# Two transformer blocks on one core: the order of rotary, convolutions and weight splits ahead of the scan loop

## The reference

```python
hn = rmsnorm_2(x, norm_mix_g[layer])
proj = hn @ w_in[layer]
u_pool, m_q, m_k, m_v, m_o, m_i, m_f, a_q, a_k, a_v = jnp.split(proj, offsets, axis=-1)
y_pool = pool_mixer(u_pool, pool_w[layer], pool_scale[layer])
y_mlstm = mlstm_mixer(m_q, m_k, m_v, m_o, m_i + gb[:n_gate], m_f + gb[n_gate:],
                      mlstm_conv_w[layer], mlstm_norm_g[layer])
y_attn = attn_mixer(a_q, a_k, a_v, q_norm_g[layer], k_norm_g[layer], cos, sin)
x = x + jnp.concatenate([y_pool, y_mlstm, y_attn], axis=-1) @ w_out[layer]
x = x + mem_cross_attn(rmsnorm_2(x, norm_mem_g[layer]), mem, ca_wq[layer], ca_wkv[layer], ca_wo[layer])
x = x + ec_moe(rmsnorm_2(x, norm_ffn_g[layer]), router_w[layer], expert_w_gu[layer], expert_w_down[layer])
```

## Time and profile before

| | |
|---|---|
| median of 3 runs | 1495.85 us (1495.27 to 1496.95) |
| profiled execution | 1495.81 us |
| its span | 1494.0 us |
| busy: PE, PEld | 1156.1, 779.3 us |
| busy: DVE, ACT, POOL | 443.3, 379.1, 69.3 us |
| DMA | 503.37 MB, mean 337 GB/s |

### The profile page before, as it was taken

How to read it: one execution, slowest core, us unless ns; L and a number is a source line. 1 busy time by engine, 2 the same in 40 slices (tenths; PEclk the granted TensorE clock), 3 DMA queues, 4 the chain that set the end, 5 groups by cost and what they waited for, 6 DMA issues and landing times.

```text
span 1494.0 us, 20251 instructions
## 1 busy us (share of the span) xinstructions
PE 1156.1 (77%) x8876; PEld 779.3 (52%) x8876; DVE 443.3 (30%) x879; ACT 379.1 (25%) x836; POOL 69.3 (5%) x83
## 2 busy tenths in 40 slices
PE   9999999999998997897556567566665665675677
PEld 8998989999976875442223223223222232232234
DVE  5555777545678854010000000000000000000002
ACT  5655566444555644110000000000000000000002
POOL 0000020000033411000000000000000000000000
PEclk9999999999998998898778787877777787877888
DMA  8435546555553388999999999999999999999996
GB/s 316 166 138 202 197 170 233 204 198 198 198 179 119 104 341 362 376 434 441 426 437 429 431 434 433 436 431 430 436 427 440 425 438 429 434 433 432 428 421 275
DMA packets 29164, 503.37 MB, mean 337 GB/s; under 512 B 4114, under 2 KB 4754, under 8 KB 8084
## 3 DMA queue, kind: packets, MB, share of 16 engines
q1 hardware_dynamic: 25200, 493.43, 79.4%
q10 hardware_dynamic: 3876, 8.65, 1.7%
HBM read 501.02 MB, written 1.05 MB: 336 GB/s over the span
## 4 chain that ended last, share of the span: by engine, by line
issue 63%; PE 31%; DVE 3%; ACT 2%; POOL 1%; DMA 0%; POOLq 0%; DVEq 0%; ACTq 0%
PE PB L99 30%; PE PB L102 1%; DVE SPL L108 1%; ACT SPH L105 1%; POOL SPL L108 0%; DVE XN L116 0%; DVE AQK L108 0%; DMA RAW<-in_wst_dram 0%; POOL SM L136 0%; POOL SP L112 0%; ACT XN L105 0%; DVE SM L128 0%; ACT SP L105 0%; DVE XQL L108 0%; DVE RT L108 0%
## 5 line engine op out<-in xcount | busy, mean ns | idle before, releaser
L99 PE MATMUL PB<-RING,XS 128*32 128x512 f32 x2048 | 297.6, 731 | 173.8 <-DMA RING<-in_wgu_dram 170.0
L99 PEld LDWEIGHTS PB<-RING,XS 128*32 128x32 f32 x2048 | 69.3, 128 | 347.3 <-DMA RING<-in_wgu_dram 185.2
L99 PE MATMUL PB<-RING,HHT 128*32 128x256 f32 x2048 | 152.3, 456 | 108.9 <-DMA RING<-in_wdn_dram 106.6
L108 DVE TENSOR_TENSOR SPL<-RAW,SPH 128x512 fp32r<-128x512 f32 x316 | 209.0, 719 | 42.3 <-ACT SPH L105 40.1
L99 PE MATMUL PB<-XTH,SPL 128*128 128x256 f32 x704 | 201.7, 287 | 0.0
L99 PE MATMUL PB<-XTH,SPH 128*128 128x256 f32 x704 | 199.2, 283 | 0.0
L99 PE MATMUL PB<-XTL,SPH 128*128 128x256 f32 x704 | 199.1, 283 | 0.0
L105 ACT ACTIVATE SPH<-RAW 128x512 fp32r<-128x512 f32 x340 | 186.8, 621 | 12.1 <-DMA RAW<-in_wst_dram 5.3
L99 PEld LDWEIGHTS PB<-RING,HHT 128*32 128x32 f32 x2048 | 72.2, 130 | 173.7 <-DMA RING<-in_wdn_dram 110.6
L105 ACT ACTIVATE SG<-PB 128x512 f32<-128x512 f32 (+1 forms) x21 | 11.9, 566 | 510.0 <-PE PB L99 508.7
L99 PEld LDWEIGHTS PB<-XTL,SPH 128*128 128x128 f32 x704 | 135.0, 192 | 0.5
(11 more groups left out here) (315 smaller groups left out, 1353.7 us busy)
## 6 DMA issues: line engine op xcount, KB each, us to landing
RAW<-in_wst_dram SPq DMA_DIRECT2D x84, 1024.0 KB, 4.8
RING<-in_wgu_dram SPq DMA_DIRECT2D x13, 2048.0 KB, 40.5
RING<-in_wgu_dram SPq DMA_DIRECT2D x14, 1024.0 KB, 9.0
RING<-in_wdn_dram SPq DMA_DIRECT2D x6, 2048.0 KB, 13.5
RING<-in_wgu_dram SPq DMA_DIRECT2D x2, 4096.0 KB, 19.5
RING<-in_wdn_dram SPq DMA_DIRECT2D x2, 4096.0 KB, 17.9
RING<-in_wdn_dram SPq DMA_DIRECT2D x3, 1024.0 KB, 42.8
RAW<-in_wst_dram SPq DMA_DIRECT2D x4, 256.0 KB, 5.6
```

Of the source, the lines that this page charges most:

```text
L99: return pe.do(lambda e: e.matmul(out_, lhsT, rhs, start=start, stop=stop), after)
L108: return on.do(lambda e: e.tensor_tensor(out_, a, b, op), after)
```

## The change

The tiles SP_ of the first two (step 0 and 2) move over AQK, those of the others to 139 and 141 KB. The generator `conv` now stops ahead of its tanh and once more at its end. Blocks 0 and 2 are convolved together, behind the first tile of the product for u and v; their tanh is emitted behind the copies of the second tile and of the transposes. Blocks 1 and 3 follow in step 0 of the loop, behind `attn_norm`. Three calls of `bg(4, 2)` are gone, one stands behind the first convolutions' end, and `bg(4, 1)` in the loop is `bg(6, 2)`. The exponentials of step 0 don't wait for `qk_ok[3]` any more.

```diff
--- before.py
+++ after.py
@@ -242,7 +242,7 @@
     BC = place("BC", [P, T], F32, at(194))
     MS = place("MS", [P, T], F32, at(195))
     NAC = place("NAC", [P, 2, P], F32, at(196))
-    SP_ = [place(f"SP{i}", [P, 512], F32, at(135 + 2 * i)) for i in range(4)]
+    SP_ = [place(f"SP{i}", [P, 512], F32, at(kb)) for i, kb in enumerate((151.5, 153.5, 139, 141))]
     ST_ = [place(f"ST{i}", [P, 512], F32, at(119 + 2 * i)) for i in range(4)]
 
     CQ = place("CQ", [P, 4, T], F32, at(119))
@@ -1090,21 +1090,20 @@
         for j in range(1, 5):
             c = [stt(CO[:, b, :], CI[:, b, j:j + T], CW[:, b, j:j + 1], CO[:, b, :], ALU.mult, ALU.add, ci)
                  for b, ci in zip(bs, c)]
+        yield
         a = [act(QK[:, b, :], CO[:, b, :], ACT.Tanh, ci, ffn_done, scale=0.5) for b, ci in zip(bs, c)]
         for b, ai in zip(bs, a):
             qk_ok[b] = stt(QK[:, b, :], QK[:, b, :], 1.0, CO[:, b, :], ALU.add, ALU.mult, ai)
+        yield
 
     conv_product(0)
     bg(4, 2)
     conv_product(1)
     m1, m2, mt = next(gates)
-    bg(4, 2)
     turn_qk(0, r0, (2, 3))
     conv_product(2)
     conv_product(3)
-    bg(4, 2)
     r1 = next(rot1)
-    bg(4, 2)
 
 
     def turn_gates():
@@ -1126,10 +1125,12 @@
         mv_ok.append(m)
         if t == 0:
             nac, em = turn_gates()
-            conv((0, 1))
+            conv02 = conv((0, 2))
+            next(conv02)
     xt_read = w
     turn_qk(1, r1, (2, 3))
-    conv((2, 3))
+    next(conv02)
+    bg(4, 2)
 
     ct = {}
 
@@ -1185,7 +1186,7 @@
         e = []
         for j in range(2):
             pr = SP_[2 * (i % 2) + j]
-            e += [act(pr[:, t * T:t * T + T], PB[bs[j]][:, t * T:t * T + T], ACT.Exp, d, st.get(("tr", i - 2)), qk_ok[3],
+            e += [act(pr[:, t * T:t * T + T], PB[bs[j]][:, t * T:t * T + T], ACT.Exp, d, st.get(("tr", i - 2)), qk_ok[3] if i else None,
                       scale=0.125, bias=nm[:, 2 * j + t:2 * j + t + 1], accum_out=rs[:, 2 * j + t:2 * j + t + 1])
                   for t in range(2)]
         held[bs[0]] = held[bs[1]] = e
@@ -1306,11 +1307,15 @@
         if i >= 1:
             attn_turn(i - 1)
         attn_norm(i, pool if i < 3 else dve)
+        if i == 0:
+            conv13 = conv((1, 3))
+            next(conv13)
+            next(conv13)
         scan_weights(i)
         ca_memory(i)
         if i >= 1:
             scan_values(i - 1)
-        bg(4, 1)
+        bg(6, 2)
     og = [stt(MO[:, t, :], MO[:, t, :], 1.0, NG[:, :], ALU.add, ALU.mult, mo_ok[t], c2_in) for t in range(2)][-1]
 
     def w_out2(t, n, ks):
```

## The result

| | before | changed |
|---|---|---|
| median | 1495.45 us (7 runs, 1494.66 to 1496.95) | 1499.73 us (7 runs, 1499.54 to 1501.95) |
| ratio | | 1.0025, interval 1.0016 to 1.0035 |
| profiled execution, its span | 1495.81, 1494.0 us | 1499.81, 1498.1 us |

The forecast was 1492.3 us, its range 1489.5 to 1496.8, with 0.55 on faster and 0.09 on slower. The change is slower: the interval lies above 1.

What follows compares the result with a forecast made beforehand. VectorE sets the pace until TensorE takes over in the third loop step, ahead of a DMA-bound expert stage. Terms: -9.4 + 4.8 + 1.4 - 0.7 - 0.8 + 1.0 + 0.2 = -3.5, so 1495.81 - 3.5 = 1492.3 us; range 1489.5 to 1496.8.

Steps and rivals of the forecast that it cites:

- Bound and passage to the end: Expert stage is DMA-bound and untouched; time saved ahead of the first expert matmul comes out one for one, under 6 us.
- The stretch ahead of the loop: With splits and two convolutions moved away, step 0's reductions start 9.4 us earlier, including a 1.1 us VectorE wait.
- Step 0: First loop step, now with convolutions 1 and 3 (4.8 us back on VectorE) and six split pieces; forecast about 13 us.
- the lock: Convolutions 1 and 3 on VectorE and GpSimd's normalisation blocking each other in step 0; the forecast costed it at 0.
- TensorE idles about 4 us in the long first step and may fall to 1.2 GHz ... I take 0.2: A lower clock slows TensorE's step-1 work some 2 us; VectorE sees 0 to 1.3 us, taken as 0.2.
- -0.7 for the 0.72 of before: Step 1: VectorE's 0.72 us wait for TensorE disappears because GpSimd's normalisation is long done; 0.7 us gained.
- Contention ... 0.5 us a step: GpSimd's fifth and sixth pieces overlap VectorE's last one or two splits: 0.5 us a step, 1.0 in two; bounds 0 and 6.
- the 0.8 us for GpSimd's late pieces: Step 1: GpSimd's pieces, delivered last by ScalarE, fall mostly beside the reductions, so VectorE's splits gain 0.8 us.
- In the third step that point lies ahead of the splits: TensorE takes over ahead of the third step's splits, so only steps 0 and 1 count: 1.4 us back for extra splits.
- rival 2: VectorE and GpSimd choke in the loop, all four VectorE splits overlapping GpSimd's: 4.8 us slower, 1500.6 us; chance 0.08.
- Rival 1: Convolutions and normalisation block each other in step 0, 3.9 us more: 1496.2 us, no change; 0.25 with gains lost in small waits.

Runs made afterwards that it cites:

- e7: Kernel before with only the splits moved, convolutions as before, and all low parts of moved and loop splits on VectorE: 1495.73 us, ratio 0.9995.
- e6: Changed kernel with the normalisation of step 0 on VectorE instead of GpSimd: 1501.08 us, ratio 1.0029.
- e16: Changed kernel with idle matmuls (results unused) in TensorE's gaps of step 1 alone, 16 and 8: 1493.26 us, ratio 0.9983 to the kernel before.
- e10: Changed kernel with 16 idle matmuls ahead of step 1's scan scores and 9 ahead of ca_memory(2): 1496.47 us, one execution.
- e13: Changed kernel with idle matmuls in three TensorE gaps: 16 and 8 in step 1, 9 ahead of ca_memory(2): 1496.67 us, ratio 1.0002 to the kernel before.
- e14: e1 with idle matmuls: 2 and 6 in step 0, 4 ahead of attn_turn(0), 7 ahead of ca_memory(2): 1493.26 us, ratio 0.9977 to the kernel before.
- e9: e1 with idle matmuls in step 0 only, 2 ahead of the scan scores and 6 inside them: 1495.99 us, ratio 0.9986 to the kernel before.
- e1: Kernel before with the splits moved alone, convolutions, tanh and SP_ as before: 1494.83 us, ratio 0.9984.
- e15: e1 with idle matmuls in steps 0 and 1 (2, 6 and 4), none in step 2: 1495.38 us, ratio 0.9985 to the kernel before.
- e3: Changed kernel with bg(6, 0) in the loop, all six low parts of a step on VectorE: 1495.72 us, ratio 0.9999 to the kernel before.
- e5: Changed kernel with 30 idle matmuls ahead of step 1's scan scores and 16 ahead of ca_memory(2): 1499.81 us, ratio 1.0023 to the kernel before.

## Why the prediction was wrong, step by step

- **Bound and passage to the end: right.** DMA is nearly idle ahead of the first expert matmul in the changed kernel too (a share of 0.19 and 0.21 in 598:600 and 600:602), and the stage behind it kept its length. What the chain loses or wins up to there comes out one for one, within the 2.6 us by which that stage varies over all traces (894.5 to 897.1 us).
- **The stretch ahead of the loop: right, in part by luck.** -9.9 us for the forecast -9.4. The granted clock of TensorE was 1.00 up to 486, its level of 2.4 GHz. VectorE waited 3.00 us for the tanh instead of 1.1, but reached that point 2.2 us sooner, since the last two instructions of the gates took 1.40 and 0.42 us with GpSimd idle where they had 2.66 and 1.27 beside its splits: I had not looked at what else the absent GpSimd splits would speed up. Two errors of about 2 us cancelled. Before, then changed:

```profile
458.37 2.66 DVE L131 TENSOR_TENSOR_SCAN MS<-MT 32x256 f32<-32x256 f32 x2
461.14 1.27 DVE L108 TENSOR_TENSOR MT<-MS,BC 64x256 f32<-64x256 f32 x1
...
459.64 1.40 DVE L131 TENSOR_TENSOR_SCAN MS<-MT 32x256 f32<-32x256 f32 x2
461.14 0.42 DVE L108 TENSOR_TENSOR MT<-MS,BC 64x256 f32<-64x256 f32 x1
```
- **Step 0: mis-sized by 1.3 us** (+7.3 for 6.0). The largest part is a tiny tensor_scalar, 1.15 us at 476.24 beside a GpSimd split, and 0.17 in the kernel before and in e7, where GpSimd has no splits. With the convolutions the stretch from the reciprocal to the weights grew by 5.2 us instead of 4.8, of which the lock makes 0.8 (e6) and the rest came cheaper than forecast. Four splits took 3.56, not 3.3, and VectorE's idle 0.18 ahead of them went.
- **"TensorE idles about 4 us in the long first step and may fall to 1.2 GHz ... I take 0.2": this step failed.** The gap was 4.07 us, as said, and the clock fell, as said possible. I priced it by VectorE's direct wait and took the low end of 0 to 1.3. What it costs is that wait and all that follows from it: slow matmuls (4.1 us for ca_memory(1)), VectorE's wait of 1.94 us where the sum had it gone (-0.7 for the 0.72 of before), splits caught beside GpSimd's, and the second gap and fall. Removing the falls in the same kernel is worth 5.1 us of trace (e16). Between the forecast of -3.5 and the trace's +2.9 lie 6.4, and the other 1.3 are those of step 0; that the two make up the whole is partly luck, since small errors elsewhere cancel.
- **"Contention ... 0.5 us a step" and the 0.8 us for GpSimd's late pieces failed as its consequence.** I assumed that ScalarE paces the splits, so that GpSimd's fifth and sixth come last. In steps 1 and 2 VectorE came 2 us after ScalarE's first piece, with its pieces ready, and met both of GpSimd's. What decides the price is how many VectorE splits begin behind a GpSimd split under way (e16), and that hangs on how far ahead of the end of GpSimd's normalisation VectorE comes: 2.0 us ahead the four took 2.7 or 3.8 us, 0.4 us ahead or later 4.6 (e10, e16 against e13, e14 and the changed kernel).
- **"In the third step that point lies ahead of the splits" failed.** The CTL behind step 2's splits frees the bank of ca_memory(3), so TensorE's closing stretch starts only there: it began 0.45 us late at the attention values, and 2.3 us late at ca_memory(3), after a gap of 1.59.
- **Rivals.** The sign was rival 2's, in part its mechanism (four splits at 4.6), but its condition is not GpSimd's load, and that its 1500.6 is near the result is luck: it had VectorE at +7.1 where it was at +3.9. VectorE's CTL ahead of the last attention values held TensorE for about 0.1 us only. Rival 1 was right about the lock and not its size.

Open: why the first reduction of the second rotary comes at 447.4 to 450.0 us from one execution to the next, what the four best times of e9 look like in a trace, and by what rule a gap makes the clock fall.

## What to carry to other kernels

A saving on the engine that sets the pace is only worth what the other engines' gaps let through: where a move opens a gap of TensorE of some microseconds, price not only the gap but the matmuls behind it at half the clock, and then who waits for these. When two engines share work that slows both (here subtractions on VectorE and GpSimd), the order in which they arrive decides the price: with a wait of 0.69 us ahead of them four splits took 4.63 us (e13), without it 2.69 (e16). When a row shows no harm on one engine, read the row of the other as well. To find such circles, look for the wait that grew although its own work did not, and fill or close the gap ahead of it in an experiment of its own.

## What the runs showed of the hardware

- TensorE's clock fell to 1.2 GHz behind a gap of 4.07 us and behind one of 2.35 us (changed kernel), behind gaps of 0.38 and 1.37 us among matmuls on 64 and 40 rows (e1) and behind one of 1.51 us (e15), and did not behind 1.41 and 1.04 us in e3. It fell behind 1.65 us in e5 and not behind 1.63 in e13, and fell behind 0.98 in e9. So the length of the last gap alone does not tell. The Trainium skill, "TensorE: Matmul & The Clock Gate", section "HAM oscillation", describes a loop whose waits, for DMA there, let the clock fall anew in every round. In the changed kernel the waits were for VectorE, and the clock fell in steps 1 and 2 (0.50 in 488:490, 0.51 in 504:506) but not in steps 0 and 3.
- Four VectorE subtractions 128x512 took 2.50 to 2.70 us with GpSimd idle or at its normalisation, and 4.63 beside two of GpSimd's, where two of the four took 1.75 us each instead of 0.68; six alone took 3.69. GpSimd's four multiplications took 3.62 us without such subtractions beside them (changed kernel, steps 1 and 2) and 4.50 and 4.33 with them (e16).
- The eight scalar_tensor_tensor with two SBUF inputs took 3.25 us alone and 4.05 beside GpSimd's tensor_scalar.
- A 128x4 tensor_scalar on VectorE took 1.15 us instead of 0.17 beside a GpSimd split, though it reads one small array of SBUF. The prediction gave the rule without its exception: the Trainium skill, "SBUF — State Buffer", section "Who interferes with whom", says that an instruction with one SBUF input does not contend as long as it is outside the 2-port modes. No run shows in which mode this instruction ran.
